# Two 512-column matmuls and one of 128 in place of three of 384, and three gathered rows moved behind the sum of the first token tile

## The chip, the cores and the metric

The kernel runs on one core of one Trainium2 chip. The metric is the device time of one execution in microseconds (us). The kernel before has a median of 3558.94 us over 3 runs (3557.57 to 3561.96). All data are 32-bit floats. A core has a matrix engine (TensorE, PE in the profile, with its weight loads on a row of their own, PEld), three engines for elementwise work (VectorE = DVE, ScalarE = ACT, GpSimd = POOL), and SyncE (SP), which here only issues transfers.

## The reference, cut to what matters

The program is two blocks of a language model over 256 tokens of width 2048: a first block of convolution, gated linear attention and a mixture of 16,384 small experts (PEER), and a second block of a gated delta rule and cross attention. Only the last part of the PEER layer and the norms behind it are touched. For each token and each of 8 heads, 16 experts are picked by keys; the output is a weighted sum of the picked rows of a table V:

```python
idx = jnp.take_along_axis(cidx, pos, axis=-1)      # 8 heads x 16 picks per token, out of 128*128 experts
gate = jax.nn.softmax(top_s, axis=-1)
h = jax.nn.gelu(jnp.einsum('thkd,td->thk', U[ib], xb))
w = gb * h
y = jnp.einsum('thk,thkd->td', w, V[ib])           # V: 16384 x 2048
h = h + y
... _rmsnorm(h, normf_g), and the second block's rms_norm of that
```

## The kernel before, in words

There are two token tiles m = 0 and 1 of 128 tokens (MT = 2). The 2048 columns of the PEER output are computed in two ways at once.

Columns CD = 1152 to 2047 are done by rows. GpSimd gathers, for head and pick (256 gathers, `vgs`, six slots, GS = 6), one row of V per token, 128 x 896 each, and VectorE multiplies it by the pick's weight and adds it to the residual `h_tok` (line 2080). Each of these counts `vg_used`.

Columns 0 to 1151 are done dense. The weights w have been spread into a matrix of 128 tokens x 16,384 experts for each token tile (`weights_of[m]`), and TensorE multiplies it by all of V's first 1152 columns. The product runs over 128 blocks i of 128 experts (NKEY = 128). `dense(i, m)` (line 1545) does one block for one token tile: three matmuls of 384 columns (VW = 384), all three with the same weights, accumulated in three PSUM banks over all i. The weights are read as `weights_of[m][:, i // LO, :, i % LO]` with the last axis 16 long (LO = 16), so 128 values that lie 16 floats (64 bytes) apart. The blocks of V come through five slots `vds` (VS = 5), loaded by SyncE's queue, which waits on `vd_used`. A 32-bit matmul is executed as two passes: in the trace each has two weight loads and two matmul records.

The order on TensorE is written out by hand: 256 small products `scatter(n)` (line 1542) that spread the weights of the tokens; between them, after every 32, `dense(i, 0)` for i = 0 to 3; then for i = 0 to 122 `dense(i, 0)` (from i = 4) and `dense(i, 1)` in turn; then the last five blocks for m = 0, after which `y_dense` goes to 1, then the last five for m = 1, after which it goes to 2. Behind them stand the transposes of the normalised rows into `hT` (line 1598), with a diagonal matrix `by_row[:, m]` as the second operand. They wait for `f_by_row`.

The end of the stage: `add_dense(m)` on VectorE adds the PSUM sums to `h_tok` (lines 2036 and 2038), `gained(m, cols)` multiplies by the norm's gain (line 2042), ScalarE sums squares (`total`, line 1782) and takes roots (lines 1799 and 1801), `biases(m)` and `row_scales(m)` on VectorE make the row's scale and `by_row`. SyncE's queue, after the last block of V, loads the first five weight tiles of the next stage (`wts`, line 1318), each waiting on a count of `vg_used` (250 for the first, 254 for the other four), and then the memory values (line 1320, at 256). The next stage is behind a barrier of all engines.

Of the kernel before, what the change touches and what calls it, by code (L numbers as in the profile page):

```python
# [21 lines left out]
ALU = mybir.AluOpType  # L22
# [10 lines left out]
MT = TX // P  # L33
# [6 lines left out]
BANK = 512  # L40
# [15 lines left out]
GSUB = 16  # L56

PH, NKEY, PTOP = 8, 128, 16
CD, VW = 1152, 384
CU = 896  # L60

DH = 128
# [37 lines left out]
def build(nc, a, out):  # L100
# [30 lines left out]
    with outer:  # L131
# [3 lines left out]
        PS = outer.enter_context(nc.psum_tensor("PS", [P, BANKS, BANK], F32))  # L135
# [35 lines left out]
        def spot(at, *shape):  # L171

            return shaped(mem[:, at:at + math.prod(shape)], shape)
# [37 lines left out]
        h_tok, mem_tok = spot(0, MT, D), spot(16640, MT, D)  # L211
# [838 lines left out]
        HN, US, GS, VS, OS, LO = MT * PH, 6, 6, 5, 4, 16  # L1050
        CG, GU, KU, UT, BANKS_U, PG, PB = D - CD, D - CU, CU // P, 4, 4, 5, 3
        W0, W1 = ring_spot(0, NKEY // LO, P, LO), spot(4096, NKEY // LO, P, LO)
        weights_of = (W0, W1)
# [5 lines left out]
        def xn_t(k):  # L1059
            return xnD[:, k, :] if k < KU else xnR[:, k - KU, :]  # L1060
# [31 lines left out]
        vds = [spot(22272 + (GS - 2) * CG + s * CD if s < VS0 else MEM + (GS1 - GS0) * CG, CD) for s in range(VS)]  # L1092
# [33 lines left out]
        def turned_rows(k):  # L1126
            return PS[:, turn_bank[k // 2], (k % 2) * TX:(k % 2 + 1) * TX]
# [65 lines left out]
        with phase() as c:  # L1193
# [28 lines left out]
            with nc.Block() as block:  # L1222
# [145 lines left out]
                def _(pe):  # L1368
# [77 lines left out]
                    for h in range(PH):  # L1446
                        s = h % RING
                        pe.wait_ge(slot_loaded[s], 16 * (G_WQ // RING + 1 + h // RING))
                        for side in range(2):
                            n = 2 * h + side  # L1450
# [4 lines left out]
                            for k in range(KT):  # L1455
                                if n == 0:
                                    if k in (4, 8):
                                        h_transposes(2 * RING - 2 + k // 8)
                                    if k % 2 == 0:
                                        pe.wait_ge(ht_out, k + 2)  # L1460
                                last = nc.tensor.matmul(PS[:, n % 4, 0:TX], ring[:, s, k, side * P:(side + 1) * P], xn_t(k),
                                                        start=(k == 0), stop=(k == KT - 1))
# [5 lines left out]
                    for i in range(NKEY):  # L1468
# [5 lines left out]
                        for k in range(KU):  # L1474
                            last = nc.tensor.matmul(PS[:, i % BANKS_U, 0:TX], Ut[i % UT][:, k * P:(k + 1) * P], xnD[:, k, :],  # L1475
                                                    start=(k == 0), stop=(k == KU - 1))
# [4 lines left out]
                    for m in range(MT):  # L1481
                        for side in range(2):
                            last = nc.tensor.transpose(PS[:, 5, (2 * m + side) * P:(2 * m + side + 1) * P], keys[:, m, side, :],
                                                       ident[:, :])
# [60 lines left out]
                    def dense(i, m):  # L1545

                        pe.wait_ge(vd_in[i % VS], 16 * (i // VS + 1))
                        if i == 0:
                            pe.wait_ge(w_out, NKEY // 4 * (m + 1))
                            pe.wait_ge(kv_taken, 2 * NKV)  # L1550
                        for at in range(0, CD, VW):
                            to = PS[:, 2 * m + at // VW if at < 2 * VW else 4 + m, 0:VW]
                            last = nc.tensor.matmul(to, weights_of[m][:, i // LO, :, i % LO], vds[i % VS][:, at:at + VW],  # L1553
                                                    start=(i == 0), stop=(i == NKEY - 1))
                        return last

# [30 lines left out]
                    for m in range(MT):  # L1587
                        for i in range(NKEY - VS, NKEY):
                            last = dense(i, m)
                        last.then_inc(y_dense, 1)  # L1590

                    for m in range(MT):
                        pe.wait_ge(f_by_row, m + 1)
                        for k in range(KT):
                            if m == 0 and k in (0, 10):

                                pe.wait_ge(y_added, 2 if k == 0 else 4)
                            last = nc.tensor.matmul(turned_rows(k)[:, m * P:(m + 1) * P], y_tok[:, m, k * P:(k + 1) * P],
                                                    by_row[:, m, :], start=True, stop=True)
# [4 lines left out]
                def _(act):  # L1604
# [173 lines left out]
                    def total(n, src, m, cols):  # L1778
                        if squares[0]:
                            act.wait_ge(f_squares, squares[0])  # L1780
                        squares[0] += 1
                        nc.scalar.activation(junk[:, cols], src[:, m, cols], ACT.Square,
                                             accum_out=ssf[:, n, m:m + 1]).then_inc(f_squares, 1)

                    by_rows, by_dense = slice(CD, D), slice(0, CD)
                    for m in range(MT):

                        act.wait_ge(vg_used, PH * PTOP * (m + 1))
                        act.wait_ge(y_ready, m + 1)
                        total(0, h_tok, m, by_rows)  # L1790
                        total(2, y_tok, m, by_rows)
                    for m in range(MT):
                        act.wait_ge(y_added, 2 * m + 2)
                        total(1, h_tok, m, by_dense)
                        act.wait_ge(y_ready, MT + m + 1)
                        total(3, y_tok, m, by_dense)
                        act.wait_ge(f_squares, 2 * MT + 2 * m + 2)
                        act.wait_ge(f_chain, 4 * m + 3)
                        nc.scalar.activation(ssf[:, ROOT2, m:m + 1], ssf[:, 3, m:m + 1], ACT.Sqrt, bias=ssf[:, BIAS2, m:m + 1],
                                             scale=1.0 / D).then_inc(f_roots, 1)  # L1800
# [7 lines left out]
                def _(dve):  # L1808
# [75 lines left out]
                    for m in range(MT):  # L1884
                        hc = h_tok[:, m, CU:D]
# [110 lines left out]
                    for n in range(HN):  # L1996
                        runs = beside.get(n, ())
                        steps = itertools.chain.from_iterable(search(later) for later in runs)
                        for j in range(PTOP):
                            at = n * PTOP + j  # L2000
                            m, h = divmod(n, PH)
# [30 lines left out]
                        one_hots(n)  # L2032
                    def add_dense(m):
                        dve.wait_ge(y_dense, m + 1)
                        hc = h_tok[:, m, 0:2 * VW].rearrange("p (b n) -> p b n", n=VW)
                        nc.vector.tensor_tensor(hc, hc, PS[:, 2 * m:2 * m + 2, 0:VW], ALU.add).then_inc(y_added, 1)
                        hc = h_tok[:, m, 2 * VW:CD]
                        nc.vector.tensor_tensor(hc, hc, PS[:, 4 + m, 0:VW], ALU.add).then_inc(y_added, 1)
                        dve.wait_ge(y_added, 2 * m + 2)

                    def gained(m, cols):
                        nc.vector.tensor_tensor(y_tok[:, m, cols], h_tok[:, m, cols], frow[:, cols], ALU.mult).then_inc(y_ready, 1)
# [2 lines left out]

                    def biases(m):
                        one = slice(m, m + 1)
                        dve.wait_ge(f_squares, 2 * MT + 2 * m + 1)
                        nc.vector.tensor_scalar(ssf[:, MEAN1, one], ssf[:, 1, one], ssf[:, 0, one], 1.0 / D, ALU.add,
                                                ALU.mult).then_inc(f_chain, 1)  # L2050
                        dve.wait_ge(f_chain, 4 * m + 1)
                        nc.vector.tensor_scalar(ssf[:, BIAS1, one], ssf[:, MEAN1, one], EPS, EPS, ALU.add, ALU.mult).then_inc(f_chain, 1)
                        dve.wait_ge(f_chain, 4 * m + 2)
                        nc.vector.scalar_tensor_tensor(ssf[:, BIAS2, one], ssf[:, 2, one], 1.0 / D, ssf[:, BIAS1, one],
                                                       ALU.mult, ALU.add).then_inc(f_chain, 1)

                    def row_scales(m):
                        dve.wait_ge(f_roots, m + 1)
                        nc.vector.reciprocal(ssf[:, SCALE2, m:m + 1], ssf[:, ROOT2, m:m + 1]).then_inc(f_chain, 1)
                        dve.wait_ge(f_chain, 4 * m + 4)  # L2060
                        nc.vector.tensor_scalar(by_row[:, m, :], ident[:, :], ssf[:, SCALE2, m:m + 1], None,
                                                ALU.mult).then_inc(f_by_row, 1)

                    by_rows, by_dense = slice(CD, D), slice(0, CD)
                    dve.wait_ge(h_back, 16)
                    dve.wait_ge(w_ready, MT)
                    for n in range(HN):
                        m, h = divmod(n, PH)
                        for j in range(PTOP):
                            at = n * PTOP + j  # L2070
                            hc = h_tok[:, m, CD:D]
                            if n == HN - 1 and j == 0:

                                dve.wait_ge(f_in, 16)
                                dve.wait_ge(vd_used, 100)
                                gained(0, by_rows)
                            dve.wait_ge(vg_in[at % GS], 16 * (at // GS + 1))
                            if at:
                                dve.wait_ge(vg_used, at)
                            nc.vector.scalar_tensor_tensor(hc, vgs[at % GS], dots[:, m, h * PTOP + j:h * PTOP + j + 1], hc,  # L2080
                                                           ALU.mult, ALU.add).then_inc(vg_used, 1)
                    dve.wait_ge(vg_used, HN * PTOP)
                    dve.wait_ge(vd_used, 112)
                    gained(1, by_rows)
                    add_dense(0)
                    gained(0, by_dense)
                    biases(0)
                    row_scales(0)
                    add_dense(1)
                    gained(1, by_dense)  # L2090
                    biases(1)
# [64 lines left out]
        for i in range(NG):  # L2156
# [6 lines left out]
            at = done = 0  # L2163
# [1153 lines left out]
```

## Time and profile before

| | |
|---|---|
| median of 3 runs | 3558.94 us |
| the profiled execution's own time | 3557.57 us |
| its span, first to last instruction | 3555.8 us |
| PE busy | 3495.7 us (98%) |
| DVE, ACT, POOL busy | 60%, 18%, 29% |
| line 1553 (the dense products), two groups, PE busy | 268.6 + 267.4 us |
| dense products from the first to the last pass | 1946.6 to 2469.2 us of the span |

The profile is of one execution. Busy time of PE overlaps from one matmul to the next, because a matmul's record lasts until its results are out; the distance between two starts is what a matmul costs in a stream. A group's mean duration is therefore longer than its cost: 486 ns for a 384-column pass, while the passes of this line start 322 to 323 ns apart.

### The profile page before, as it was taken

What the parts mean: (1) busy time and instruction counts of PE and PEld (TensorE: products, weight loads), DVE (VectorE), ACT (ScalarE), POOL (GpSimd) and SP (SyncE); (2) the same over time, 40 slices, a digit from 0 to 9 for tenths busy, and PEclk for the clock granted to TensorE, in tenths of its full rate; (3) what the DMA queues carried; (4) which work ended last, traced back from release to release, by engine and by line L of the source; (5) the groups of instructions that cost most, each with busy time, mean ns of one, the idle gap of its engine ahead of it and who ended that gap; (6) DMA issues with size and microseconds to landing.
All of it is one profiled execution on the core that took longest, in us unless ns stands there. A gap on an engine that the chain in (4) does not pass through costs nothing. (4 is left out here: it accounts for less than half of the span.)

```text
span 3555.8 us, 51079 instructions
## 1 busy us (share of the span) xinstructions
PE 3495.7 (98%) x20690; PEld 3183.0 (90%) x20690; DVE 2147.3 (60%) x4178; ACT 635.4 (18%) x1425; POOL 1025.5 (29%) x797
## 2 busy tenths in 40 slices
PE   8999999999999999999999999999999999999999
PEld 7878887899998888888888999998999999999988
DVE  4884102145555389966798766665366766766653
ACT  0002202100001212222367200001222122222100
POOL 0000100010000045555586788884000121122000
PEclk9999999999999999999999999999999999999999
DMA  6434432244454589999997799998334322221452
GB/s 223 142 130 142 142 134 95 104 159 173 173 220 189 225 295 401 404 408 409 351 342 278 281 408 404 408 408 329 120 142 155 119 100 89 92 101 72 159 201 103
DMA packets 159591, 785.05 MB, mean 221 GB/s; under 512 B 19540, under 2 KB 21484, under 8 KB 123644
## 3 DMA queue, kind: packets, MB, share of 16 engines
q1 hardware_dynamic: 101112, 510.14, 38.3%
q0 software_dynamic: 57344, 268.47, 19.5%
q10 hardware_dynamic: 900, 3.17, 0.3%
q8 instruction: 165, 2.70, 0.3%
q14 instruction: 70, 0.57, 0.0%
HBM read 771.06 MB, written 10.64 MB: 220 GB/s over the span
## 5 line engine op out<-in xcount | busy, mean ns | idle before, releaser
L424 PE MATMUL PS<-mem,ring 128*128 128x272 f32 (+1 forms) x2816 | 646.8, 392 | 1.2 <-DVE mem L938 1.2
L424 PEld LDWEIGHTS PS<-mem,ring 128*128 128x128 f32 x2816 | 541.1, 193 | 104.6 <-issue 6.0
L1334 POOL DMA_INDIRECT mem<-in_peer_ug,idx x256 | 328.9, 1285 | 557.1 <-DVE idx L1950 335.5
L1363 POOL DMA_INDIRECT mem<-in_peer_vg,idx x256 | 380.4, 1486 | 105.2 <-issue 82.4
L2080 DVE SCALAR_TENSOR_TENSOR mem<-mem 128x896 f32<-128x896 f32 x256 | 294.8, 1152 | 177.4 <-DMA mem<-in_peer_vg,idx 176.8
L2003 DVE CUSTOM_DVE_ANT_0 mem<-mem 128x1152 f32<-128x1152 f32 x256 | 349.3, 1366 | 81.1 <-DMA mem<-in_peer_ug,idx 80.1
L1475 PE MATMUL PS<-mem 128*128 128x256 f32 x1792 | 387.5, 379 | 1.2 <-DMA mem<-in_peer_ud 1.2
L1475 PEld LDWEIGHTS PS<-mem 128*128 128x128 f32 x1792 | 340.2, 190 | 48.2 <-DMA mem<-in_peer_ud 2.0
L432 PEld LDWEIGHTS PS<-mem,ring 128*128 128x128 f32 x3136 | 350.3, 192 | 0.1
L432 PE MATMUL PS<-mem,ring 128*128 128x128 f32 x3136 | 350.3, 275 | 0.0
L2384 POOL TENSOR_TENSOR mem<-mem,ring 128x512 f32<-128x512 f32 x84 | 114.8, 1381 | 693.6 <-DVE mem L3127 512.9
L2431 PE MATMUL PS<-mem,ring 128*128 128x128 f32 x2560 | 312.3, 275 | 0.9 <-issue 0.6
L2431 PEld LDWEIGHTS PS<-mem,ring 128*128 128x128 f32 x2560 | 299.0, 192 | 1.7 <-issue 0.6
L1553 PE MATMUL PS<-mem,ring 128*128 128x384 f32 x768 | 268.6, 487 | 0.3 <-DMA mem<-in_peer_vd 0.3
L1553 PE MATMUL PS<-mem 128*128 128x384 f32 x768 | 267.4, 486 | 0.0
L1553 PEld LDWEIGHTS PS<-mem 128*128 128x128 f32 x768 | 226.1, 294 | 21.8
L1553 PEld LDWEIGHTS PS<-mem,ring 128*128 128x128 f32 x768 | 226.0, 295 | 21.6 <-DMA mem<-in_peer_vd 0.8
L2431 PE MATMUL PS<-mem 128*128 128x128 f32 x1920 | 238.8, 276 | 3.9 <-DVE ring L2948 3.9
L2431 PEld LDWEIGHTS PS<-mem 128*128 128x128 f32 x1920 | 226.0, 192 | 4.9 <-DVE ring L2948 4.7
L960 DVE SCALAR_TENSOR_TENSOR mem<-mem 128x256 f32<-128x256 f32 x480 | 192.2, 476 | 0.0
L353 POOL TENSOR_TENSOR mem<-mem 128x1024 f32<-128x1024 f32 x3 | 7.1, 2357 | 487.3 <-PE PS L537 326.7
L1517 PE MATMUL PS<-mem 128*128 128x256 f32 x512 | 120.1, 382 | 2.5 <-ACT mem L1716 1.5
(439 smaller groups left out, 4476.2 us busy)
## 6 DMA issues: line engine op xcount, KB each, us to landing
ring<-in_first_tiles SPq DMA_DIRECT2D x143, 1024.0 KB, 4.8
ring<-in_dn_tiles SPq DMA_DIRECT2D x88, 1024.0 KB, 5.1
mem<-in_peer_vd SPq DMA_DIRECT2D x128, 576.0 KB, 7.8
mem<-in_peer_ud SPq DMA_DIRECT2D x128, 448.0 KB
ring<-in_out_panels SPq DMA_DIRECT2D x16, 2048.0 KB, 9.3
ring<-in_w_out SPq DMA_DIRECT2D x8, 2048.0 KB, 11.7
ring<-in_peer_wq SPq DMA_DIRECT2D x8, 2048.0 KB, 10.2
mem<-second_keys SPq DMA_DIRECT2D x64, 256.0 KB
```

Of the source, the lines that this page charges most:

```text
L424: last = nc.tensor.matmul(PS[:, 4 + n % 4, 0:T if wide else TX], wslots[slot_of[n]][:, k, :], x, start=(k == 0), stop=(k == KT - 1))
L432: last = nc.tensor.matmul(PS[:, bank, at * P:(at + 1) * P], w[:, k, :], x[:, k, :], start=(k == 0), stop=(k == KH2 - 1))
L960: ins = nc.vector.scalar_tensor_tensor(dst, src, w, acc[:, j % 4, :], ALU.mult, ALU.add)
L1334: nc.gpsimd.indirect_dma_start(ugs[at % US], None, a["peer_ug"], bass.IndirectOffsetOnAxis(ap=idx[:, n, j:j + 1], axis=0)).then_inc(u_in[a ...
L1363: nc.gpsimd.indirect_dma_start(vgs[at % GS], None, a["peer_vg"], bass.IndirectOffsetOnAxis(ap=idx[:, n, j:j + 1], axis=0)).then_inc(vg_in[ ...
L1475: last = nc.tensor.matmul(PS[:, i % BANKS_U, 0:TX], Ut[i % UT][:, k * P:(k + 1) * P], xnD[:, k, :], start=(k == 0), stop=(k == KU - 1))
L1517: last = nc.tensor.matmul(PS[:, KVB[side], 0:PW], x, y, start=(k == 0), stop=(k == KT - 1))
L1553: last = nc.tensor.matmul(to, weights_of[m][:, i // LO, :, i % LO], vds[i % VS][:, at:at + VW], start=(i == 0), stop=(i == NKEY - 1))
L2003: nc.vector.tensor_tensor_reduce(out=ugs[at % US], in0=ugs[at % US], in1=h_tok[:, m, CU:D], scale=1.0, scalar=0.0, op0=ALU.mult, op1=ALU.a ...
L2080: nc.vector.scalar_tensor_tensor(hc, vgs[at % GS], dots[:, m, h * PTOP + j:h * PTOP + j + 1], hc, ALU.mult, ALU.add).then_inc(vg_used, 1)
L2384: nc.gpsimd.tensor_tensor(No[:, m, :, :], NT_[:, m, :, :], lev[:, l:l + 1, :].broadcast_to([P, VG, P]), ALU.mult).then_inc(no_ready, 1)
L2431: ins = nc.tensor.matmul(to, w[:, k, :], y[:, k, :], start=(k == 0 and group in (0, 2, 3)), stop=(k == GROUP - 1), skip_group_check=True)
```

## The change

The three matmuls of `dense` are cut at other columns: 512, 512 and 128 instead of 384, 384 and 384. Each of the first two fills a whole PSUM bank. `add_dense` follows with 1024 and 128 columns instead of 768 and 384.

On VectorE, the sum, the gain, the biases and the row scales of token tile 0 move from behind the last gathered row to between the last rows: `add_dense(0)` and `gained(0, by_dense)` stand ahead of the third last row, `biases(0)` ahead of the second last and `row_scales(0)` ahead of the last. ScalarE now does all sums of tile 0 before those of tile 1, and the counts waited for follow. A wait for `vd_used` 112 ahead of `gained(1, by_rows)` goes.

```diff
-CD, VW = 1152, 384
+CD = 1152
@@ dense(i, m), TensorE
-                        for at in range(0, CD, VW):
-                            to = PS[:, 2 * m + at // VW if at < 2 * VW else 4 + m, 0:VW]
-                            last = nc.tensor.matmul(to, weights_of[m][:, i // LO, :, i % LO], vds[i % VS][:, at:at + VW],
+                        for at in range(0, CD, BANK):
+                            w = min(BANK, CD - at)
+                            to = PS[:, 2 * m + at // BANK, :] if w == BANK else PS[:, 4 + m, 0:w]
+                            last = nc.tensor.matmul(to, weights_of[m][:, i // LO, :, i % LO], vds[i % VS][:, at:at + w],
                                                     start=(i == 0), stop=(i == NKEY - 1))
@@ ScalarE
                     for m in range(MT):
 
                         act.wait_ge(vg_used, PH * PTOP * (m + 1))
-                        act.wait_ge(y_ready, m + 1)
+                        act.wait_ge(y_ready, 2 * m + 1)
                         total(0, h_tok, m, by_rows)
                         total(2, y_tok, m, by_rows)
-                    for m in range(MT):
                         act.wait_ge(y_added, 2 * m + 2)
                         total(1, h_tok, m, by_dense)
-                        act.wait_ge(y_ready, MT + m + 1)
+                        act.wait_ge(y_ready, 2 * m + 2)
                         total(3, y_tok, m, by_dense)
...
@@ VectorE, add_dense
-                        hc = h_tok[:, m, 0:2 * VW].rearrange("p (b n) -> p b n", n=VW)
-                        nc.vector.tensor_tensor(hc, hc, PS[:, 2 * m:2 * m + 2, 0:VW], ALU.add).then_inc(y_added, 1)
-                        hc = h_tok[:, m, 2 * VW:CD]
-                        nc.vector.tensor_tensor(hc, hc, PS[:, 4 + m, 0:VW], ALU.add).then_inc(y_added, 1)
+                        hc = h_tok[:, m, 0:2 * BANK]
+                        nc.vector.tensor_tensor(hc, hc, PS[:, 2 * m:2 * m + 2, :].rearrange("p b n -> p (b n)"),
+                                                ALU.add).then_inc(y_added, 1)
+                        hc, w = h_tok[:, m, 2 * BANK:CD], CD - 2 * BANK
+                        nc.vector.tensor_tensor(hc, hc, PS[:, 4 + m, 0:w], ALU.add).then_inc(y_added, 1)
@@ VectorE, the loop over the gathered rows
                                 gained(0, by_rows)
+                            if n == HN - 1 and j == PTOP - 3:
+                                add_dense(0)
+                                gained(0, by_dense)
+                            if n == HN - 1 and j == PTOP - 2:
+                                biases(0)
+                            if n == HN - 1 and j == PTOP - 1:
+                                row_scales(0)
...
                     dve.wait_ge(vg_used, HN * PTOP)
-                    dve.wait_ge(vd_used, 112)
                     gained(1, by_rows)
-                    add_dense(0)
-                    gained(0, by_dense)
-                    biases(0)
-                    row_scales(0)
                     add_dense(1)
```

TensorE's row in the program where the scatter products end and the dense blocks begin to follow each other, before (`x3` is three instructions, each of two passes; `mem,ring` is a block of token tile 0, `mem` one of tile 1):

```order
L1542 MATMUL PS<-mem 128x128 x32
L1553 MATMUL PS<-mem,ring 128x384 x3
L1542 MATMUL PS<-mem 128x128 x32
L1553 MATMUL PS<-mem,ring 128x384 x3
L1553 MATMUL PS<-mem 128x384 x12
L1553 MATMUL PS<-mem,ring 128x384 x3
L1553 MATMUL PS<-mem 128x384 x3
```

The same place after, where line 1554 is the matmul that was on line 1553:

```order
L1542 MATMUL PS<-mem 128x128 x32
L1554 MATMUL PS<-mem,ring 128x512 x2
L1554 MATMUL PS<-mem,ring 128x128
L1542 MATMUL PS<-mem 128x128 x32
L1554 MATMUL PS<-mem,ring 128x512 x2
L1554 MATMUL PS<-mem,ring 128x128
L1554 MATMUL PS<-mem 128x512 x2
L1554 MATMUL PS<-mem 128x128
```

Nothing moved on TensorE; each of the 256 blocks of three equal instructions is now two long ones and a short one, and behind each short one stands a long one of the next block (or, four times, a scatter product).

VectorE's end of the stage, before:

```order
L2080 SCALAR_TENSOR_TENSOR mem<-mem 128x896 x16
L2042 TENSOR_TENSOR mem<-mem 128x896
L2036 TENSOR_TENSOR mem<-mem,PS 128x768
L2038 TENSOR_TENSOR mem<-mem,PS 128x384
L2042 TENSOR_TENSOR mem<-mem 128x1152
L2049 TENSOR_SCALAR mem<-mem 128x1
L2052 TENSOR_SCALAR mem<-mem 128x1
L2054 SCALAR_TENSOR_TENSOR mem<-mem 128x1
L2059 RECIPROCAL mem<-mem 128x1
L2061 TENSOR_SCALAR mem<-ident,mem 128x128
```

VectorE's same stretch after, up to the sum of tile 1 (line 2088 is the gathered row, 2043 the gain, 2036 and 2039 the sums):

```order
L2088 SCALAR_TENSOR_TENSOR mem<-mem 128x896 x13
L2036 TENSOR_TENSOR mem<-mem,PS 128x1024
L2039 TENSOR_TENSOR mem<-mem,PS 128x128
L2043 TENSOR_TENSOR mem<-mem 128x1152
L2088 SCALAR_TENSOR_TENSOR mem<-mem 128x896
L2050 TENSOR_SCALAR mem<-mem 128x1
L2053 TENSOR_SCALAR mem<-mem 128x1
L2055 SCALAR_TENSOR_TENSOR mem<-mem 128x1
L2088 SCALAR_TENSOR_TENSOR mem<-mem 128x896
L2060 RECIPROCAL mem<-mem 128x1
L2062 TENSOR_SCALAR mem<-ident,mem 128x128
L2088 SCALAR_TENSOR_TENSOR mem<-mem 128x896
```

The wait for `y_dense` 1, which stood behind all 256 rows, stands behind 253 of them, and the last three rows and the gain of tile 1's row columns now follow it.

## Rows read from the trace of the kernel before

**Rows 1.** The page, part 1: busy time of each engine, share of the span, instructions.
```profile
PE 3495.7 (98%) x20690; PEld 3183.0 (90%) x20690; DVE 2147.3 (60%) x4178; ACT 635.4 (18%) x1425; POOL 1025.5 (29%) x797
```

**Rows 2.** Stretches of the whole core: length, then busy us of each engine, PEclk, DMA share, GB/s.
```profile
1981.00:2452.00 471.00, 470.71 (x1460) 429.50 (x1459) 293.74 (x256) 2.29 (x5) 373.51 (x250) 1.00 1.01 404
```

**Rows 3.** Line 1553 alone in one stretch of 325 us: PE and PEld busy with passes, PEclk, DMA, GB/s.
```profile
2014.50:2339.57 325.07, 325.07 (x1009) 296.92 (x1008) 1.00 1.02 407
```

**Rows 4.** Timeline, PE, 512-column passes: start us, us, engine, line, op, shapes, passes, idle before.
```profile
701.94 1.88 PE L536 MATMUL PS<-mem 128*128 128x512 f32 x4
703.66 0.59 PE L537 MATMUL PS<-mem,ring 128*128 128x512 f32 x1
```

**Rows 5.** Timeline, PE, 128-column passes with weights that lie side by side.
```profile
1796.59 1.06 PE L1499 MATMUL PS<-mem 128*128 128x128 f32 x8
1797.48 1.89 PE L1517 MATMUL PS<-mem 128*128 128x256 f32 x8
```

**Rows 6.** Groups of weight loads by shape: line, op, shape, count, busy us, mean ns, idle.
```profile
L1553 PEld LDWEIGHTS PS<-mem 128*128 128x128 f32 x768 | 226.1, 294 | 21.8
L1553 PEld LDWEIGHTS PS<-mem,ring 128*128 128x128 f32 x768 | 226.0, 295 | 21.6 <-DMA mem<-in_peer_vd 0.8
L2596 PEld LDWEIGHTS PS<-mem 128*128 128x128 f32 x576 | 69.6, 192 | 0.0
L2495 PEld LDWEIGHTS PS<-mem 128*56 128x56 f32 x32 | 4.1, 130 | 5.1 <-issue 2.5
```

**Rows 7.** Groups of PE in 0.1 us around two first passes of a dense block, and one within.
```profile
L1553 PE MATMUL PS<-mem,ring 128*128 128x384 f32 x1 | 0.6, 589 | 0.0
L1553 PE MATMUL PS<-mem,ring 128*128 128x384 f32 x1 | 0.6, 593 | 0.0
L1553 PE MATMUL PS<-mem,ring 128*128 128x384 f32 x1 | 0.5, 486 | 0.0
```

**Rows 8.** Timeline, PE, a dense block behind scatter products.
```profile
1957.43 2.21 PE L1553 MATMUL PS<-mem,ring 128*128 128x384 f32 x6
1959.47 0.61 PE L1542 MATMUL PS<-mem 128*128 128x128 f32 x4
```

**Rows 9.** The end of the stage, timeline of all engines.
```profile
2450.50 2.63 SPq L1318 DMA_DIRECT2D ring<-in_dn_tiles  x5
2451.64 1.09 DVE L2042 TENSOR_TENSOR mem<-mem 128x896 f32<-128x896 f32 x1
2452.81 0.95 ACT L1782 ACTIVATE mem<-mem 128x896 f32<-128x896 f32 x1 [26.78 <-DVE mem L2042]
2453.18 0.43 SPq L1320 DMA_DIRECT2D mem<-memory_values  x1
2453.89 0.95 ACT L1782 ACTIVATE mem<-mem 128x896 f32<-128x896 f32 x1
...
2459.75 0.95 DVE L2036 TENSOR_TENSOR mem<-mem,PS 128x768 f32<-128x768 f32 x1 [7.01 <-PE PS L1553]
2460.62 0.55 DVE L2038 TENSOR_TENSOR mem<-mem,PS 128x384 f32<-128x384 f32 x1
2461.20 1.36 DVE L2042 TENSOR_TENSOR mem<-mem 128x1152 f32<-128x1152 f32 x1
2464.41 0.29 DVE L2061 TENSOR_SCALAR mem<-ident,mem 128x128 f32<-128x128 f32 x1
2469.22 3.73 PE L1598 MATMUL PS<-mem 128*128 128x128 f32 x32
2469.42 0.95 DVE L2036 TENSOR_TENSOR mem<-mem,PS 128x768 f32<-128x768 f32 x1 [4.73 <-PE PS L1553]
2474.42 3.84 PE L1598 MATMUL PS<-mem 128*128 128x128 f32 x32 [1.47 <-DVE mem L2061]
```

**Rows 10.** The page, part 5: the gathered rows on VectorE.
```profile
L2080 DVE SCALAR_TENSOR_TENSOR mem<-mem 128x896 f32<-128x896 f32 x256 | 294.8, 1152 | 177.4 <-DMA mem<-in_peer_vg,idx 176.8
```

**Rows 11.** Timeline, PE, the next stage's first use of the five weight tiles.
```profile
2491.17 4.05 PE L2397 MATMUL PS<-mem,ring 128*128 128x256 f32 x18
```

More of the change, by code:

```diff
@@ L1788, in _ @@
                         act.wait_ge(vg_used, PH * PTOP * (m + 1))
-                        act.wait_ge(y_ready, m + 1)
+                        act.wait_ge(y_ready, 2 * m + 1)
                         total(0, h_tok, m, by_rows)
                         total(2, y_tok, m, by_rows)
-                    for m in range(MT):
                         act.wait_ge(y_added, 2 * m + 2)
                         total(1, h_tok, m, by_dense)
-                        act.wait_ge(y_ready, MT + m + 1)
+                        act.wait_ge(y_ready, 2 * m + 2)
                         total(3, y_tok, m, by_dense)
-                        act.wait_ge(f_squares, 2 * MT + 2 * m + 2)
+                        act.wait_ge(f_squares, 4 * m + 4)
                         act.wait_ge(f_chain, 4 * m + 3)
@@ L2047, in biases @@
                         one = slice(m, m + 1)
-                        dve.wait_ge(f_squares, 2 * MT + 2 * m + 1)
+                        dve.wait_ge(f_squares, 4 * m + 3)
                         nc.vector.tensor_scalar(ssf[:, MEAN1, one], ssf[:, 1, one], ssf[:, 0, one], 1.0 / D, ALU.add,
```

## The prediction

> **What bounds the kernel now.** The page comes first: PE is busy for 98% of the span [rows 1]. The row by engine and stretch for 1981 to 2452 us, where the dense blocks stand, says the same of the stage that is changed: PE 470.71 of 471.00 us, DVE 293.74, and the granted clock 1.00, which is the level of 2.4 GHz [rows 2]. So every nanosecond that a pass of a dense block gains or loses is a nanosecond of the result. It is only 0.3 us in 471 that PE stands still there. The DMA engines are full too (share 1.01, 404 GB/s) [rows 2], but the one that waits for them is VectorE with its gathered rows (177.4 us) [rows 10]. Next the price of a pass. With 1008 passes of 384 columns in 325.07 us a pass costs 322.5 ns [rows 3], a block of six 1.935 us, and the 256 blocks 495.4 us. The question is what the same 1152 columns cost when they are cut 512, 512, 128. I read that from passes of these widths elsewhere, and from the weight loads, because each pass has its own.
>
> **The columns.** Four passes of 512 columns take 1.72 us from the first start to the start of what follows, 0.430 us each [rows 4]. Eight passes of 128 columns take 0.89 us, 0.111 us each [rows 5]. A block becomes 4 x 0.430 + 2 x 0.111 = 1.942 us against 1.935, so +7 ns, and 256 of them +1.8 us. The starts are rounded to 10 ns, so I take +1.5 us and keep 1 to 2.
>
> **The weight loads.** This is the term that decides. A weight load of 128 columns takes 192 ns in a stream of short passes, a load of 56 columns 130 ns [rows 6]. The 72 columns between them are worth 62 ns, 0.86 ns each, so 128 columns are about 110 ns of reading and 82 ns are fixed. 110 ns is also the distance of the 128-column passes [rows 5]: there a load and a pass are equally long and neither shows. The weight loads of line 1553 take 294 and 295 ns [rows 6]. Their 128 values lie 64 bytes apart in memory, the others side by side. With the same fixed 82 ns the reading takes 212 ns. Behind a pass of 322 ns that is covered. Behind a pass of 111 ns, 212 - 110 = 102 ns of it can't be.
>
> The trace has this very case four times. Where the first pass of a dense block stands behind a 128-column scatter pass, its weight load runs beside that short pass, and the matmul's record is 589 and 593 ns long (591 in the two others) where all the rest are 486 [rows 7]: 103 to 107 ns more, mean 105. In the timeline that block lasts from 1957.43 to 1959.47, 2.04 us [rows 8], against 6 x 322.5 ns = 1.935: again +105 ns. It isn't a transfer or a semaphore, since the rows of the block show no idle time before them. I take 105 ns for each strided load that stands beside a 128-column pass.
>
> Now count. In a new block the order of passes is 512, 512, 512, 512, 128, 128. The load of the second 128-column pass runs beside the first, and the load of the next block's first pass runs beside the second. Both are strided. That is two per block and 512 in all. For four blocks (i = 0 to 3 of tile 0) a scatter product with contiguous weights comes next, and behind the last block nothing that is strided: 507 are left. 507 x 0.105 = 53.2 us. The four exposures that are there today, before those four blocks, stay.
>
> The Trainium skill has a rule against this term. TensorE: Matmul & The Clock Gate, section "LDWEIGHTS (loading the stationary operand)", gives the load as P / 1.2 ns with P the number of columns, which is 107 ns for 128, with nothing on how far apart the values lie. By that rule the sum would be the +1.5 us of the columns alone. The 294 ns of line 1553 beside the 192 ns of another line with as many columns speak against it [rows 6].
>
> **The sums on VectorE.** 768 columns take 0.95 us and 384 take 0.55 [rows 9]: 0.40 us for 384 columns and 0.15 fixed. So 1024 cost 1.22 and 128 cost 0.28, together 1.50 as before. Term: 0, at most 0.1 either way.
>
> **The moved steps.** Before, VectorE is through with its 256 rows at 2452.7 and waits 7.01 us for tile 0's sum [rows 9]. Now it stops three rows earlier and does them behind the sum. From the start of that sum to the end of the row scales tile 0's chain takes 2464.70 - 2459.75 = 4.95 us [rows 9]; three rows of 1.15 [rows 10] and the gain of 1.09 [rows 9] make 9.5 us in all, if the waits for ScalarE in that chain are not even filled. It must be over when tile 1's sum can start. That was 9.67 us later (2469.42 - 2459.75) and will be 5 x 2.15 = 10.8 us later, because the five blocks of tile 1 are longer. It fits with 1.3 us to spare. ScalarE then has two sums of squares of 1.08 us each (2452.81 to 2453.89) [rows 9] that it did before the wait until now. They end at 9.5 + 2.2 = 11.7 us at the latest, and the next one waits for the second sum of PSUM at 10.8 + 1.45 = 12.2. It fits with 0.5 us. Tile 0's `by_row` was ready at 2464.70, and PE takes it at 2469.22 [rows 9]; now it comes one or two rows later, with still over 2 us left. So nothing is gained and nothing lost: on the path are only the last block, tile 1's sum and its 5.0 us to the second group of transposes (2469.42 to 2474.42) [rows 9], which stay. Term: 0, and +0.5 at worst.
>
> **The transfers behind it.** The loads of four of the next stage's weight tiles and of the memory values wait for rows 254 and 256, so they go from 18.7 us ahead of PE's last dense pass (2450.50) [rows 9] to about 6 us ahead of it. 5 MB at the 404 GB/s of that stage [rows 2] need 13 us and end some 7 to 9 us behind it. PE wants the first tile at 2491.17, 22 us behind it [rows 11]. 13 us of cover are left. POOL has issued all gathers by row 250, since a gather waits only for the row six before it. Before that, slower dense blocks take less of the DMA's bandwidth and VectorE's rows come sooner, which helps no one, since PE is the last.
>
> **Sum.** 1.5 + 53.2 + 0 + 0 = +54.7 us. On the profiled execution's 3557.57 us that is 3612.3; its span is 3555.8, and the 1.8 us around it stay. That execution lies 1.4 us under the median of 3558.94, so the forecast for the median is 3613.6, rounded 3614.
>
> **The rivals.** (A) The loads are hidden: the queue of PE begins the load of the pass after next during a 512-column pass, so that the short passes find their weights in place. Then only the columns count, 3558.94 + 1.5 = 3560.4, no change, and this is the side on which I would be wrong altogether. For it speaks that the columns are the same in number. Against it speaks that a load overlaps one pass only in the rows that I have: before each of the four long records there was a whole row of scatter products, and the load was still late. This also holds the skill's rule. Chance 0.05. (B) Only one of the two loads shows, because the two passes of a 32-bit matmul take their weights in another way than two instructions do: 253 to 256 exposures, +27 us, 3587. The four records in the trace are all first passes of an instruction, so nothing there shows a second pass behind a short one. But the six loads of a block are alike in length. Chance 0.05. (C) The loads beside short passes cost more than the four show, because the DMA engines are full in this stage (share 1.01) and were not in the stretch of the scatter products. The price for a load late by another 20 ns would be 507 x 0.02 = +10 us, 3624. Against it, the loads average 294 and 295 ns over all 1536 [rows 6], nearly all of them in the full stage. Chance 0.05. (D) The moved steps overrun: VectorE's three rows or ScalarE's two sums end behind tile 1's sum. It decides from 1.3 us of delay on, and costs what exceeds it, 1 to 3 us more on top of the forecast, 3616. Chance 0.05; it changes the number little. The forecast itself has 0.80.
>
> **Range and chances.** A difference of 0.2% (7 us) is about what a measurement of this kernel tells from none. The forecast's own ends are 102 ns with 1 us (3558.9 + 52.7) and 107 ns with 2 us and 0.5 for the tail (3558.9 + 56.7), 3611 to 3616. For 8 in 10 I widen it to 3606 to 3621, which takes in (D) and a smaller form of (C), and leaves out (A), (B) and the far end of (C). Slower holds the forecast, (B), (C), (D): 0.94. Same holds (A): 0.05. Faster has no mechanism in the profile: 0.01.
>
> **What would show it.** In the changed profile the dense line's 128-column passes should start 215 to 218 ns apart where a strided load is beside them, not 111, and the first 512-column pass of each block should follow its 128-column pass by as much. A pair of blocks should take 4.30 us in place of 3.87, and PE should look busy all the same, for the delay is inside the records. The last dense pass should end about 55 us later. VectorE should wait for the sum of tile 0 with three rows left and, again, for that of tile 1. The forecast is wrong if the short passes start 111 ns apart.

## The result, and the profile after

| | before | after |
|---|---|---|
| median | 3560.45 us (4 runs, 3557.57 to 3564.17) | 3616.64 us (4 runs, 3615.73 to 3623.68) |
| profiled execution, its span | 3557.57, 3555.8 us | 3614.91, 3613.2 us |
| ratio, after to before | | 1.0162 (95%: 1.0144 to 1.0179) |

The changed kernel is 56 us slower, 1.6%. The forecast was 3614, in 3606 to 3621.

The page of the changed kernel, part 1, against [rows 1]:

```profile
PE 3554.3 (98%) x20690; PEld 3150.0 (87%) x20690; DVE 2145.7 (59%) x4178; ACT 635.2 (18%) x1425; POOL 1020.6 (28%) x797
```

PE's busy time rises by 58.6 us and its share stays 98%, with the same 20690 passes; DVE, ACT and POOL do what they did. So the loss is in how long the passes take. The stretch of line 1554, the dense products, that answers to [rows 3] (length, PE and PEld busy with passes, granted clock, DMA share, GB/s):

```profile
2014.50:2339.57 325.07, 325.07 (x908) 244.84 (x907) 1.00 1.02 407
```

In the same 325.07 us there are 908 passes in place of 1009, at the same granted clock of 1.00. One busy figure is the same, 325.07, and can't tell the two apart; the count can. The groups of PE by shape (count, busy, mean ns, idle before), then the weight loads, as in [rows 6]:

```profile
L1554 PE MATMUL PS<-mem 128*128 128x512 f32 x512 | 254.8, 620 | 0.0
L1554 PE MATMUL PS<-mem 128*128 128x128 f32 x256 | 62.3, 325 | 0.0
```
```profile
L1554 PEld LDWEIGHTS PS<-mem 128*128 128x128 f32 x768 | 218.7, 301 | 67.9
```

A 512-column pass elsewhere is recorded with 592 ns and a 128-column pass mostly with 272 to 276; here the means are 620 and 325. Two passes across the end of one block show why (the same view, for 0.1 us):

```profile
L1554 PE MATMUL PS<-mem 128*128 128x512 f32 x1 | 0.7, 703 | 0.0
L1554 PE MATMUL PS<-mem,ring 128*128 128x128 f32 x1 | 0.4, 380 | 0.0
```

The second 128-column pass has 380 ns (the first 273), and the next block's first 512-column pass has 703. These are 107 and 110 ns more than such passes have elsewhere, and they answer to the 589 and 593 in place of 486 in [rows 7]. (380 + 273) / 2 is 327 against the group's 325, and (703 + 3 x 593) / 4 is its 620, so the other blocks are like this one. The timeline of PE where the blocks follow each other:

```profile
1991.68 2.31 PE L1554 MATMUL PS<-mem,ring 128*128 128x512 f32 x6
1993.83 2.31 PE L1554 MATMUL PS<-mem 128*128 128x512 f32 x6
```

A block starts every 2.15 us. Before it was 1.935 [rows 3]. The end of the stage, against [rows 9]:

```profile
2404.75 1.09 DVE L2043 TENSOR_TENSOR mem<-mem 128x896 f32<-128x896 f32 x1 [5.45 <-PE PS L1554]
```
```profile
2504.01 16.28 SPq L1318 DMA_DIRECT2D ring<-in_dn_tiles  x5
...
2514.33 1.22 DVE L2036 TENSOR_TENSOR mem<-mem,PS 128x1024 f32<-128x1024 f32 x1 [90.03 <-PE PS L1554]
2515.47 0.28 DVE L2039 TENSOR_TENSOR mem<-mem,PS 128x128 f32<-128x128 f32 x1
2520.09 1.15 DVE L2088 SCALAR_TENSOR_TENSOR mem<-mem 128x896 f32<-128x896 f32 x1
2521.26 0.33 SPq L1320 DMA_DIRECT2D mem<-memory_values  x1
2521.27 1.09 DVE L2043 TENSOR_TENSOR mem<-mem 128x896 f32<-128x896 f32 x1
2523.52 0.95 ACT L1783 ACTIVATE mem<-mem 128x896 f32<-128x896 f32 x1
2524.87 3.74 PE L1599 MATMUL PS<-mem 128*128 128x128 f32 x32
2525.07 1.22 DVE L2036 TENSOR_TENSOR mem<-mem,PS 128x1024 f32<-128x1024 f32 x1 [2.71 <-PE PS L1554]
...
2530.07 3.84 PE L1599 MATMUL PS<-mem 128*128 128x128 f32 x32 [1.47 <-DVE mem L2062]
```

The last dense block ends at 2524.87 and not at 2469.22. The first dense pass is at 1948.27, in a part before it that has not changed and that took 1.65 us longer in this execution (1946.62 before); the granted clock between 1700 and 1735 us was 0.90 here and 1.00 before, which may be the reason. From the first pass to the transposes the stage takes 2524.87 - 1948.27 = 576.60 us against 522.60: +54.0. From there to the second group of transposes it is 5.20 us in both (2530.07 - 2524.87, and 2474.42 - 2469.22).

The next stage's first use of the weight tiles, against [rows 11]:

```profile
2536.25 8.77 PE L2498 MATMUL PS<-mem 128*56 128x256 f32 x32 [2.33 <-PEq L119]
2548.51 3.83 PE L2400 MATMUL PS<-mem,ring 128*128 128x256 f32 x17
```

It is 23.64 us behind the last dense block and was 21.95. These 1.7 us are in the product with 56 columns of weights (line 2498), 8.77 us here and 7.08 in the timeline of before:

```profile
2480.59 7.08 PE L2495 MATMUL PS<-mem 128*56 128x256 f32 x32 [2.34 <-PEq L119]
```

The granted clock over this product tells the two apart. The whole core in its stretch, here and then before (length, busy us of PE, PEld, DVE, ACT and POOL, granted clock, DMA share, GB/s):

```profile
2536.25:2545.00 8.75, 8.75 (x33) 4.81 (x33) 2.53 (x2) 1.89 (x1) 7.57 (x18) 0.81 0.57 240
```
```profile
2480.59:2487.60 7.01, 7.00 (x32) 4.05 (x32) 2.53 (x2) 1.91 (x1) 6.17 (x13) 1.00 0.54 224
```

A clock of 0.81 over 8.75 us is full speed less 0.19 x 8.75 = 1.66 us. It isn't the change: experiment 4, with neither the cut nor the moved steps, has 8.70 us at 0.81, and experiment 2, with the moved steps, has 7.08 at 1.00. PE stood still for 2.33 or 2.34 us just before the product in all four, so why the clock fell in two of them no run tells. So 57.3 us between the two profiled executions are 1.65 + 54.0 + 1.7, and only the 54.0 are the change.

### The profile page after: what moved, and what is told of

It reads as the page before. It is cut to its first block and busy times, and to the rows that moved or that the text cites. A ratio compares the mean times of both kernels' runs of the same rounds, so it can differ in the third digit from the quotient of the medians.

```text
span 3613.2 us, 51078 instructions
## 1 busy us (share of the span) xinstructions
PE 3554.3 (98%) x20690; PEld 3150.0 (87%) x20690; DVE 2145.7 (59%) x4178; ACT 635.2 (18%) x1425; POOL 1020.6 (28%) x797
## 3 DMA queue, kind: packets, MB, share of 16 engines
q0 software_dynamic: 57344, 268.47, 19.2%
## 5 line engine op out<-in xcount | busy, mean ns | idle before, releaser
L1334 POOL DMA_INDIRECT mem<-in_peer_ug,idx x256 | 359.1, 1403 | 533.5 <-DVE idx L1950 335.3
L1363 POOL DMA_INDIRECT mem<-in_peer_vg,idx x256 | 350.8, 1370 | 110.4 <-issue 74.7
L1554 PE MATMUL PS<-mem,ring 128*128 128x512 f32 (+1 forms) x768 | 295.3, 521 | 0.0
L1554 PE MATMUL PS<-mem 128*128 128x512 f32 (+1 forms) x768 | 295.1, 522 | 0.0
```

Source lines behind the costliest of these rows:

```text
L1334: nc.gpsimd.indirect_dma_start(ugs[at % US], None, a["peer_ug"], bass.IndirectOffsetOnAxis(ap=idx[:, n, j:j + 1], axis=0)).then_inc(u_in[a ...
L1363: nc.gpsimd.indirect_dma_start(vgs[at % GS], None, a["peer_vg"], bass.IndirectOffsetOnAxis(ap=idx[:, n, j:j + 1], axis=0)).then_inc(vg_in[ ...
```

## The experiments

Each ratio is to the kernel before, run beside it, with its 95% interval. Experiments 3, 4, 7, 8, 10 and 11 read other values of the same tiles as weights, so their dense columns are other numbers; they are kernels for measuring only. The kernel before had medians of 3562.58, 3563.57 and 3563.04 us beside experiments 1 to 4, 5 to 8 and 9 to 11. For the dense stage I use the first and the last start of a dense pass, which the view of one line gives.

| kernel | median us | ratio | first to last dense pass |
|---|---|---|---|
| before | 3560.45 | | 1946.6 to 2468.9: 522.3 |
| after | 3616.64 | 1.0162 (1.0144 to 1.0179) | 1948.3 to 2524.7: 576.4 |
| 1: cut only | 3613.84 | 1.0145 (1.0128 to 1.0162) | 1947.4 to 2523.8: 576.4 |
| 2: moved steps only | 3562.53 | 1.0002 (0.9993 to 1.0012) | 1948.7 to 2471.7: 523.0 |
| 3: changed kernel, weights side by side | 3563.60 | 1.0001 (0.9992 to 1.0011) | 1954.2 to 2478.9: 524.7 |
| 4: kernel before, weights side by side | 3562.94 | 1.0000 (0.9991 to 1.0010) | 1954.2 to 2476.2: 522.0 |
| 5: cut 512, 384, 256 | 3566.53 | 1.0008 (0.9998 to 1.0018) | 1947.9 to 2472.8: 524.9 |
| 6: cut 512, 448, 192 | 3591.82 | 1.0077 (1.0060 to 1.0094) | 1953.2 to 2503.8: 550.6 |
| 7: weights 8 bytes apart | 3562.16, one run | | 1947.6 to 2473.7: 526.1 |
| 8: 16 bytes apart | 3627.38, one run | | 1954.9 to 2538.8: 583.9 |
| 9: moved steps, nine rows | 3574.40 | 1.0031 (1.0019 to 1.0042) | 1956.3 to 2478.3: 522.0 |
| 10: 12 bytes apart | 3590.63, one run | | 1947.6 to 2502.1: 554.5 |
| 11: 32 bytes apart | 3624.99, one run | | 1948.2 to 2534.6: 586.4 |

**1 and 2: which half of the change.** From the changed kernel, experiment 1 takes back this and all that goes with it, and experiment 2 the cut:

```diff
 # 1
-                            if n == HN - 1 and j == PTOP - 3:
-                                add_dense(0)
-                                gained(0, by_dense)
...
+                    add_dense(0)
+                    gained(0, by_dense)
+                    biases(0)
+                    row_scales(0)
                     add_dense(1)
 # 2
-                        for at in range(0, CD, BANK):
+                        for at in range(0, CD, VW):
```

> Only the columns are cut 512, 512, 128; the steps of the end stay where they were before. Theory (a weight load of values 64 bytes apart does not fit beside a 128-column pass): the whole loss is here, 54 to 56 us over the kernel before, a dense block of 2.150 us. Rival (the moved steps cause a part of it): less than 54 us, the rest in the run with the steps alone.

> Only the steps of the end are moved; the columns stay 384, 384, 384. Theory: no change, 0 within 1 us, since tile 0's chain and the three rows need about 8.4 to 9.5 us and tile 1's five blocks last 9.67 us. Rival (the moved steps overrun tile 1's sum): VectorE's gain of tile 1 or ScalarE's sums end behind it, and 1 to 3 us are lost. Rival (the moved steps are what costs in the change): tens of us slower.

The whole loss is in the cut: the stage has 576.4 us with or without the moved steps, and 523.0 with them alone. Experiment 1 as a whole is 51.3 us over its kernel before, 3 us under the 54 to 56 that I expected and 5 under the 56.2 of the whole change. No trace gives these 5 us to the moved steps: the stage is 576.4 us in both, from the last dense pass to the end of the span it is 1088.6 and 1088.5 us, and experiment 2 is at 1.0002. The intervals of the two ratios overlap. The steps are neutral, as their tail shows. The timeline of experiment 2 (line 2035 is tile 0's and tile 1's sum, 2041 the gain, 1782 the sum of squares):

```profile
2462.51 0.95 DVE L2035 TENSOR_TENSOR mem<-mem,PS 128x768 f32<-128x768 f32 x1 [12.81 <-PE PS L1553]
2469.45 1.09 DVE L2041 TENSOR_TENSOR mem<-mem 128x896 f32<-128x896 f32 x1
2471.70 0.95 ACT L1782 ACTIVATE mem<-mem 128x896 f32<-128x896 f32 x1
2472.18 0.95 DVE L2035 TENSOR_TENSOR mem<-mem,PS 128x768 f32<-128x768 f32 x1 [1.64 <-PE PS L1553]
2477.18 3.06 PE L1598 MATMUL PS<-mem 128*128 128x128 f32 x25 [1.47 <-DVE mem L2060]
```

VectorE is through at 2470.54, 8.03 us after it began, and waits 1.64 us for tile 1's sum; ScalarE is through with its squares at 2472.7, ahead of the next at 2473.64. The steps have 1.6 us of room on one engine and under 1 us on the other.

**3 and 4: the load, with all else equal.**

```diff
-weights_of[m][:, i // LO, :, i % LO]
+weights_of[m][:, i // LO, 8 * (i % LO):8 * (i % LO + 1), :].rearrange("p n l -> p (n l)")
```

> The changed kernel, but the dense products read as weights 128 values that lie side by side (other values of the same tile, so the dense columns of the output are other numbers). Nothing else differs. Theory: the weight load falls from 295 to about 192 ns, fits beside the 128-column pass, and the loss of 55 us goes but for 1 to 2 us: 0 to 2 us over the kernel before. Rival (short passes or full PSUM banks cost by themselves, whatever the load): it stays about 55 us slower.

> The kernel before with the same other weights, side by side (again other numbers in the dense columns). Theory: the loads get 100 ns shorter and nobody notices, since they are covered by passes of 322 ns: 0, or 0.4 us less for the four blocks behind scatter products. Rival (the loads with a stride also slow the passes beside them, by their reads of the memory): several us faster.

With the short pass kept and the weights read side by side, the loss is gone. That other values are read doesn't matter: experiments 8 and 11 read others too and are no faster than the changed kernel. The groups of experiment 3, loads and passes:

```profile
L1554 PEld LDWEIGHTS PS<-mem 128*128 128x128 f32 x768 | 135.5, 191 | 122.5 <-issue 122.5
```
```profile
L1554 PE MATMUL PS<-mem 128*128 128x512 f32 x512 | 240.9, 593 | 0.0
L1554 PE MATMUL PS<-mem 128*128 128x128 f32 x256 | 49.2, 274 | 0.0
```

Loads of 191 ns, and passes of 593 and 274 as everywhere. The stage is 2.4 us longer than before, near the columns' +1.5; PE also waited 0.9 us for blocks of V (0.3 before). Experiment 4 is the control: the same shorter loads gain nothing where they were covered. Neither short passes nor full banks cost by themselves, and the strided reads don't slow the passes that run beside them.

**5 and 6: how long the pass must be.**

```diff
-for at in range(0, CD, VW):
-    to = PS[:, 2 * m + at // VW if at < 2 * VW else 4 + m, 0:VW]
-    ... vds[i % VS][:, at:at + VW]
+for b, at, w in ((2 * m, 0, 512), (2 * m + 1, 512, 384), (4 + m, 896, 256)):   # 6: 448 and 192
+    ... PS[:, b, 0:w] ... vds[i % VS][:, at:at + w]
```

> The kernel before with its three matmuls of a dense block cut 512, 384, 256. Theory: what counts is the pass that a strided load stands beside; a 256-column pass takes 216 ns and the load needs 218 (111 ns of a contiguous one and the 107 ns that the changed profile shows on top), so 2 ns show, 507 times: 0 to 2 us. Rival (every unequal cut, or a full bank, costs): 27 us or more.

> The same with 512, 448, 192. Theory: a 192-column pass is 163 ns (160 for the columns and 2.5), the load needs 218: 55 ns show, 507 times, 28 us slower, half of the change's loss. Rival (it is a penalty of 128-column passes alone): no change. Rival (a fixed penalty for a load that doesn't fit): 54 us.

The dense blocks in the timeline of 5, then of 6:

```profile
2101.45 2.11 PE L1552 MATMUL PS<-mem 128*128 128x512 f32 x6
2103.39 2.11 PE L1552 MATMUL PS<-mem,ring 128*128 128x512 f32 x6
2105.34 1.03 PE L1552 MATMUL PS<-mem 128*128 128x512 f32 x2
```
```profile
2100.86 2.21 PE L1552 MATMUL PS<-mem 128*128 128x512 f32 x6
2102.91 2.21 PE L1552 MATMUL PS<-mem,ring 128*128 128x512 f32 x6
2104.96 1.46 PE L1552 MATMUL PS<-mem 128*128 128x512 f32 x3
```

1.945 us a block in 5, and 2.05 in 6, where before had 1.935 and after 2.15. The stage grew by 2.6 us and 28.3 us; 0 to 2 and 28 were expected, so experiment 5 is a little over its range (its median is 3.0 us over the kernel before). The rise is as long as the part of the load that sticks out of the pass, not a fixed penalty and not a matter of 128 columns.

**7, 8, 10, 11: how far apart the weights may lie.** The changed kernel, with `s` = 2, 4, 3 and 8 floats:

```diff
-weights_of[m][:, i // LO, :, i % LO]
+weights_of[m][:, i // LO, 0:8 * s, :].rearrange("p n l -> p (n l)").rearrange("p (n s) -> p n s", s=s)[:, :, i % s]
```

> The changed kernel with weights that lie 2 floats (8 bytes) apart, other values of the same tile, so the dense columns of the output are other numbers. It asks from which distance on a load takes longer. By the Trainium skill (SBUF: State Buffer, section on the DMA port swizzle, its note on 16-byte lines), two reads of one line run at full speed: weight loads of about 192 ns and the time of the kernel before. If any distance costs, loads of about 295 ns and 55 us more.

> The same with weights 4 floats (16 bytes) apart, so that each lies on another 16-byte line. By the note's demand for two reads per line: slow loads, about 295 ns, and 55 us. By its list, in which 4 floats are still free: 192 ns and the time of the kernel before. No expectation of mine between the two.

> The changed kernel with weights 3 floats (12 bytes) apart (other values of the same tile: other numbers in the dense columns). Three reads of four lie on a new 16-byte line. If a line with a single read is what costs, the load lies between the 196 ns of 2 floats and the 309 of 4, nearer to the latter, and shows in part: 20 to 55 us over the kernel before. If the boundary is a distance over 8 bytes, it is like 4 floats, 60 us.

> The changed kernel with weights 8 floats (32 bytes) apart (other values of the same tile). Weights 64 bytes apart took 291 to 299 ns to load, 16 bytes apart 309. If distance beyond a line makes no difference and 309 was that one run's, 291 to 299 again and the time of the changed kernel; if the banks of the memory matter, a number between or beside them.

The weight loads of line 1554 for tile 1 in these four, 8, 12, 16 and 32 bytes apart (count, ns min/median/max, first and last start):

```profile
L1554 PEld LDWEIGHTS PS<-mem x768: 195/196/197, 1981.5 to 2473.6; 128*128 128x128 f32 x192
```
```profile
L1554 PEld LDWEIGHTS PS<-mem x768: 250/251/264, 1981.9 to 2502.0; 128*128 128x128 f32 x192
```
```profile
L1554 PEld LDWEIGHTS PS<-mem x768: 308/309/332, 1989.5 to 2538.7; 128*128 128x128 f32 x192
```
```profile
L1554 PEld LDWEIGHTS PS<-mem x768: 312/314/338, 1983.1 to 2534.5; 128*128 128x128 f32 x192
```

190 ns side by side, 196 at 8 bytes, 251 at 12, 309 at 16, 314 at 32, and mostly 291 to 299 at 64, the kernel's own. 8 bytes are nearly free, 12 cost half, 16 and more cost all. For 12 bytes I had expected a load nearer to 309 than to 196; it is in the middle. The Trainium skill (SBUF — State Buffer, section "Door 1: The DMA port swizzle", the note on 16-byte lines) says that two reads have to hit a line for full speed and also lists a distance of 4 floats as free. The first half agrees with these loads. The second doesn't: at 4 floats the load took 309 ns and the kernel 3627.38 us. At 12 bytes two reads of every four are alone on their line of 16 bytes and two share one, and the load has half of what it has at 16 bytes over side by side (61 of 119 ns). So the reads that are alone would be what costs, and not, as my expectation counted, the three of four that begin a new line. This is worked out from one run and not tested further. Each stage follows from its load: (251 - 190) ns x 507 = 31 us on top of experiment 3's 524.7 is 555.6, measured 554.5; (309 - 190) x 507 = 60 gives 585.0, measured 583.9; 196 gives 527.7, measured 526.1; 314 gives 587.6, measured 586.4. At 64 bytes the sum fits less well: with the median load of 298 ns it gives 579.5, measured 576.4. Experiments 7, 8, 10 and 11 are single runs, but the distances between them are tens of us.

**9: how near the moved steps are to costing.** From experiment 2:

```diff
-if n == HN - 1 and j == PTOP - 3:     # the sum and the gain; then - 2 the biases, - 1 the row scales
+if n == HN - 1 and j == PTOP - 9:     # then - 8, - 7
```

> The kernel with 384, 384, 384 and the moved steps, but moved 6 rows further ahead, so that nine gathered rows stand behind the sum of tile 0 in place of three. It asks how near the moved steps are to costing. With three rows VectorE was through 8.03 us after the start of tile 0's sum. Theory: each further row is 1.18 us, so 15.1 us, against 9.67 us until tile 1's sum can start: VectorE is 5.4 us late, ScalarE's two sums of squares make it 6.1, and the second group of transposes and all behind it come 6 us later, +0.17%. Rival (the rows are taken up elsewhere, or the second group isn't what sets the end): no change, VectorE late and PE not.

Measured +11.4 us (0.31%), near double what I expected. The timeline of it:

```profile
2469.14 0.95 DVE L2035 TENSOR_TENSOR mem<-mem,PS 128x768 f32<-128x768 f32 x1 [24.15 <-PE PS L1553]
2473.82 1.59 POOL L1363 DMA_INDIRECT mem<-in_peer_vg,idx  x1 [26.75 <-DVE mem L2086]
2478.61 2.40 PE L1598 MATMUL PS<-mem 128*128 128x128 f32 x20
2483.79 1.15 DVE L2086 SCALAR_TENSOR_TENSOR mem<-mem 128x896 f32<-128x896 f32 x1 [2.73 <-DMA mem<-in_peer_vg,idx]
2486.16 1.15 DVE L2086 SCALAR_TENSOR_TENSOR mem<-mem 128x896 f32<-128x896 f32 x1 [1.21 <-DMA mem<-in_peer_vg,idx]
2488.35 0.95 DVE L2035 TENSOR_TENSOR mem<-mem,PS 128x768 f32<-128x768 f32 x1
2489.82 2.93 PE L1598 MATMUL PS<-mem 128*128 128x128 f32 x12 [8.81 <-DVE mem L2037]
2494.23 0.94 PE L1598 MATMUL PS<-mem 128*128 128x128 f32 x6 [1.48 <-DVE mem L2060]
```

VectorE begins tile 1's sum 19.2 us after tile 0's, and I had 15.1. Nearly all of the other 4.1 us are in the two rows that waited 2.73 and 1.21 us for their gather: with nine rows behind the sum the six slots don't hold them all, POOL stands still for 26.75 us until VectorE has done the first of the nine rows, the next gather starts at 2473.82, and the last three gathers start from nothing. PE then waits 8.81 us in the middle of the first group of transposes, for tile 1's sum (line 2037), which the program asks for ahead of the 11th transpose, and the second group comes 15.62 us after the first (5.20 before): +10.4. Three rows are fewer than the six slots, and in experiment 2 none of the three waited for its gather; numbers between three and nine weren't run.

## Why the prediction was right, and where its working was not

- **PE sets the time in this stage.** Right: a longer block is a longer kernel, one for one; +54.0 us in the stage, and 5.20 us behind it in both.
- **The columns, +1.5 us.** About right: 524.7 against 522.3 with side-by-side weights, of which some 0.6 us is a longer wait for blocks of V.
- **The weight loads, 507 x 105 ns = 53.2 us.** Right, and shown by undoing it alone: the changed kernel with weights side by side is at 1.0001. The size is that of the four long records of the kernel before. A block of 2.150 us is 1.942 + 0.208, so 104 ns each. Three details of the working are off and change next to nothing. The count is 508: the fourth early block of tile 0 is followed by tile 1's first block and not by a scatter product, so a scatter product stands behind a short pass three times and not four. And one dense pass of before, besides the four, is long too (696 ns); it stands where PE had waited 0.29 us for a block of V. And the chances of the forecast, (B), (C) and (D) add up to 0.95 and not to 0.94.
- **Rival A, and with it the Trainium skill's rule for a load** (TensorE: Matmul & The Clock Gate, section "LDWEIGHTS (loading the stationary operand)"), which gives 107 ns for 128 columns and names no distance, fell for weights 64 bytes apart. With 8 bytes or less between them the time that it gives is near right (3562.16 us, no loss). Rival B, only one of two loads showing, fell: both records, 380 and 703, are long. Rival C fell: 104 ns and not 125.
- **The moved steps, 0** (and rival D). Right. VectorE's room, put at 1.3 us, was 2.71 in the changed kernel (1.64 in experiment 2, where tile 1's blocks are shorter); the chain took 8.0 us and not 9.5, because the rows filled its waits. My count of the steps' cost holds while the rows behind the sum are fewer than the six slots; that condition wasn't in the prediction, and experiment 9 shows what it is worth with nine rows.
- **The transfers behind.** Right. The five tiles went out from 2504.01 to 2520.29, the memory values at 2521.26, 3.6 us ahead of the last dense block's end (I had about 6), and no one waited for them.
- **VectorE's rows come sooner.** Right: it waits for tile 0's sum from 2424.3 on, 90.03 us. It also waited 5.45 us for `vd_used` 100 at 2404.75, which I had not counted and which costs nothing.
- **The sign I called decisive was wrong.** I wrote that 128-column passes would start 215 to 218 ns apart, and that 111 ns would prove me wrong. This trace says for two of them, and then for the second of them and the pass behind it:

```profile
L1554 PE MATMUL PS<-mem,ring x3: 273/380/593, 2100.6 to 2101.1; 128*128 128x128 f32 x2, 128*128 128x512 f32 x1
```
```profile
2101.11 0.38 PE L1554 MATMUL PS<-mem,ring 128*128 128x128 f32 x1
2101.33 0.70 PE L1554 MATMUL PS<-mem 128*128 128x512 f32 x1
```

Three passes start between 2100.6 and 2101.1, and a 512-column pass is followed after 0.43 us, so the two short ones lie about 0.11 us apart. By my own words the forecast would be wrong, though its time and its cause are right. The other half of the sign held: the next block's first pass starts 0.22 us behind the second short one. A late pass is recorded from its turn on, not from when its weights are there; what grows is its duration, and the distance to the pass behind. I had this before me: the 589 ns records of [rows 7] are long, not late. The sum was right because it used their excess. The test should have been the duration or the distance between blocks.

## What to carry to other kernels

A weight load that is longer than the pass beside it shows, so count both, pass by pass; unequal cuts of the same columns leave the sum of columns alone and put two loads per block beside the shortest pass. Not all of a load's record counts: in these runs a short pass took the load's record less 81 to 83 ns (298 gave 215, 251 gave 170, 309 gave 228, each from the growth of the stage or block over 111 ns). Look at a weight load's duration before shortening a pass: at 190 ns it fits beside 128 columns of 32-bit data, at 295 it needs about 256. Work that is moved behind a wait is free only as long as the buffers in front of it hold all of its inputs.

## What the runs showed of the hardware that was not expected

- The load depends on the distance between weights, but not in proportion: 190 ns side by side, 196, 251, 309 and 314 at 8, 12, 16 and 32 bytes. At 64 bytes it is mostly 291 to 299, shorter than at 16 and 32. Why, no run tells.
- PE's busy share does not show a late weight load. Both kernels are 98% busy; beside the busy time itself, only the count of passes in a stretch, the records' mean duration and PEld's share (90% to 87%) move.
- The 13 profiled executions differ by up to 10 us ahead of the dense stage (its first pass is at 1946.6 to 1956.3 us) and by 1.7 us in one product behind it (granted clock 0.81 or 1.00), with the same code in both places. Comparing stages instead of spans takes this out: 576.4 and 576.4 us for two kernels whose medians differ by 2.8 us.
